# Four PSUM banks for the first y transposes, and one weight sum moved behind the scaling of chunk 12

## The chip, the core and the metric

The program runs on one core of a Trainium2 chip. The metric is the device time of one execution in microseconds (us); the median of the runs is what counts. The core has five engines that run their own instruction lists and meet at semaphores: TensorE (PE, matrix products and transposes into PSUM), VectorE (DVE), ScalarE (ACT), GpSimd (POOL) and SyncE (SP, which here only issues transfers).

## What is computed

One layer of a hybrid attention model on 256 tokens of width 2048, in float32. Cut to what the change touches:

```python
h = rmsnorm(x, g_norm)
proj = h @ w_in                      # q, k, v and gates of two attentions, and m_z, n_z
y_moba = rmsnorm(o_moba * silu(m_z), g_out_moba)   # 1024 columns, "half 0"
y_nsa  = rmsnorm(o_nsa  * silu(n_z), g_out_nsa)    # 1024 columns, "half 1"
y = concatenate([y_moba, y_nsa])
return rmsnorm(x + y @ w_out, g_final)
```

## The kernel before

**Products.** Each float32 product is made of three products of rounded operands: high by high, high by low, low by high (`three_products`, L647 to L649). So every block of weights is loaded by SP into one of three buffers of `w_raw`, rounded by ACT into `w_hi` (`hi`, L1022), and DVE then takes the rest into `w_lo` (`lo`, L1345). The weights are worked off in **units**: 512 rows of a chunk of 512 columns, for both halves of the tokens, 24 PE instructions of 512 columns. w_in has 15 chunks (0 to 14); w_out has 4, whose units start at number 56. A ring of three `w_hi`/`w_lo` buffers holds the rounded units, and ACT may round into one when PE has counted it as used.

**Slots.** PE, ACT and DVE each run through the same slots 0 to 75 in a loop; what an engine does in a slot, and in what order, stands in the loop's body. An engine runs ahead in its own list until a semaphore stops it. Chunks 11 to 14 (the z chunks) are worked in two pairs, (11, 12) from slot 44 on and (13, 14) from slot 52 on, with a scheme of seven block products in place of eight. Its operands are sums and differences of weight blocks, which DVE forms in `t1` to `t4`. `t4` of the second pair makes `blk_b11` from `blk_b21` (in the tile `wv`); ACT rounds it as block 6 (`block_hi`), DVE takes its rest (`block_lo`), and PE uses it in the last product of slot 53, P4.

**Around slots 51 to 53.** PE must not start the product P2 of chunk 14 into its banks before DVE has read chunk 12 out of the same banks. That is `scaled(12)`, two SCALAR_TENSOR_TENSOR instructions at L1561, after which `dve_read` lets `bank_free(14)` pass. In slot 51 DVE's order is: `t4`, `block_lo` 4, `block_lo` 5, `scaled(12)`. In slot 52 comes the `lo` of unit 51, and in slot 53 `block_lo` 6.

**The y rounds.** When a half of y has been scaled (`y_scale`, L1616), it is transposed in four rounds of four 128 by 128 transposes (`y_round_` on PE, L628, into one PSUM bank). DVE multiplies the bank by the gain into `pT` (`y_parts`, L1626, counts `yg_done`), ACT rounds it (`y_hi`, L1214), and DVE takes the rest (L1631, counts `ylo_done`). The rounds of half 0 are numbers 0 to 3; they stand in slots 55, 56, 57 and 58, and all four use the bank `b_t`, so that each waits until DVE has emptied it of the round before. Those of half 1 are numbers 4 to 7, in slots 62 and 63, in the banks `b_t`, `b_s`, `b_p`, `b_o`. Slot 58 has no unit on PE; slot 57 has unit 54, slot 59 unit 55, slot 60 unit 56. Unit 56 is the first of w_out and waits for all four rounds of half 0 (`ylo_done` 4).

The order on ACT and DVE in a slot is: round a unit of weights, then the slot's y rounds. The unit that is rounded in slots 55, 56, 57 and 58 is 54, 55, 56 and 57. DVE's `scaled(14)` and what follows from it (the sigmoid on ACT, a product of DVE, the product `xo` by z on POOL at L604, squares on ACT, `rstdy` on POOL, `y_scale(1)` on DVE) come in slots 59 to 61, and round 4 on PE in slot 62 waits for its end.

Of the kernel before, what the change touches and what calls it, by code (L numbers as in the profile page):

```python
# [20 lines left out]
S, D, P, HD = 256, 2048, 128, 128  # L21
MT = S // P
KT = D // P
NH = 8
HW = NH * HD
CW = 512
UK = 4
UPC = KT // UK
HPC = CW // HD
# [27 lines left out]
PAIRS = [(11, 12, 44), (13, 14, 52)]  # L57
# [124 lines left out]
ROUNDS = transpose_rounds()  # L182
# [20 lines left out]
JOBS = [(20 + 2 * h + i, "nsa", h, 1 - i) for h in range(8) for i in range(2)] + \  # L203
# [5 lines left out]
def score_reads(j):  # L209

    return 2 * (j + 1)
# [28 lines left out]
def heads_done(j):  # L240
# [10 lines left out]
CMP_SCORE_SLOT, CMP_TOKEN_SLOT, CMP_T_SLOT = [18, 26], [19, 27], [21, 31]  # L251
CMP_VALUES_AT = [0, 4]

Y_ROUNDS = {55: [(0, 0, 0)], 56: [(0, 0, 1)], 57: [(0, 1, 0)], 58: [(0, 1, 1)],
            62: [(1, 0, 0), (1, 0, 1)], 63: [(1, 1, 0), (1, 1, 1)]}
Y_NO = {r: n for n, r in enumerate(r for s in sorted(Y_ROUNDS) for r in Y_ROUNDS[s])}

# [8 lines left out]
def build_layer(nc, x, positions, inv_freq, w_in, g_norm, pe_ck, pe_cv, w_ck1, w_ck2, w_cv1, w_cv2,  # L266
# [4 lines left out]
    with ExitStack() as ctx:  # L271
# [7 lines left out]
        xo = sb("xo", [P, MT, D])  # L279
# [62 lines left out]
        b_s, b_o, b_t, b_p = bank("b_s"), bank("b_o"), bank("b_t"), bank("b_p")  # L342
# [29 lines left out]
        first_hi, quarters_ok, exp_done, pt_out, y_sq = sem("first_hi"), sem("quarters_ok"), sem("exp_done"), sem("pt_out"), sem("y_sq")  # L372
# [5 lines left out]
        s_read, negmax_ok, prob_ready, o_out = sem("s_read"), sem("negmax_ok"), sem("prob_ready"), sem("o_out")  # L378
        y_scaled, yg_done, ylo_done, ssf_ok, fin_dve = sem("y_scaled"), sem("yg_done"), sem("ylo_done"), sem("ssf_ok"), sem("fin_dve")
# [245 lines left out]
        def _(pe):  # L625
            def transpose4(bank_, srcs, done):
                for n, src in enumerate(srcs):
                    last = nc.tensor.transpose(bank_[:, n * P:(n + 1) * P], src, ident[:, :])  # L628
                last.then_inc(done, 1)
# [314 lines left out]
            def y_round_(r):  # L944
                half, hg, m = r
                n = Y_NO[r]
                if half == 0:
                    pe.wait_ge(y_scaled, m + 1)
                    if n == 0:
                        pe.wait_ge(t_out, len(ROUNDS))  # L950
                    bank_ = b_t
                    if n:
                        pe.wait_ge(yg_done, n)
                else:
                    pe.wait_ge(y_scaled, 2 + m + 1)
                    bank_ = (b_t, b_s, b_p, b_o)[n - 4]
                    if n == 4:
                        pe.wait_ge(yg_done, 4)
                transpose4(bank_, [xo[:, m, half * HW + (hg * HPC + h) * HD:half * HW + (hg * HPC + h + 1) * HD]
                                   for h in range(HPC)], y_round)  # L960

            def keep_busy(n):
# [370 lines left out]
        def _(dve):  # L1333
# [274 lines left out]
            def t4(p):  # L1608
                dve.wait_ge(blk_in[3], 16 * (p + 1))
                nc.vector.tensor_tensor(blk_b11, blk_b21, blk_b11, ALU.subtract).then_inc(blk_sum, 1)  # L1610
# [7 lines left out]
            def y_parts(r):  # L1618
                half, hg, m = r
                n = Y_NO[r]  # L1620
                bank_ = b_t if half == 0 else (b_t, b_s, b_p, b_o)[n - 4]
                dve.wait_ge(y_round, n + 1)
                dve.wait_ge(pt_out, len(JOBS))
                g0 = 16 + half * NH + hg * HPC
                yg = pT[:, n % 2, :].rearrange("p (h t) -> p h t", h=HPC)
                nc.vector.tensor_tensor(yg, bank_[:, :].rearrange("p (h t) -> p h t", h=HPC),  # L1626
                                        ccols[:, g0:g0 + HPC].unsqueeze(2).to_broadcast([P, HPC, P]), ALU.mult).then_inc(yg_done, 1)
                dve.wait_ge(yhi_done, n + 1)
                hi_, lo_ = ((ymT_hi, ymT_lo), (xT_hi, xT_lo))[half]
                sl = (slice(None), slice(hg * HPC, (hg + 1) * HPC), slice(m * P, (m + 1) * P))  # L1630
                nc.vector.tensor_tensor(lo_[sl], yg, hi_[sl].bitcast(F32), ALU.subtract).then_inc(ylo_done, 1)  # L1631
# [45 lines left out]
            for slot in range(NSLOT):  # L1677
                if slot == 0:
                    x_g(4)
                    x_g(5)  # L1680
                    first_lo_(1, [3])
                    first_lo_(2, [0])
                    x_lo(5)
                    first_lo_(2, [1, 2, 3])
                elif slot == 1:
                    x_g(6)
                    x_g(7)
                    lo(3)
                    x_lo(7)
                if slot == 38:  # L1690
                    x_sums()
                if slot == 40:
                    xs_residual()
                for p in range(len(PAIRS)):
                    s0 = PAIRS[p][2]
                    if slot == s0 - 4:
                        block_lo(p, 0)
                        t1(p)
                        block_lo(p, 1)
                    if slot == s0 - 2 and p:  # L1700
                        block_lo(p, 2)
                        block_lo(p, 3)
                        t3(p)
                    if slot == s0 + 1:
                        block_lo(p, 6)
                        if p:
                            z_times(PAIRS[p - 1][1])
                if slot > 1 and rounded_at(slot) is not None and rounded_at(slot) < NU:
                    lo(rounded_at(slot))
                if slot == PAIRS[0][2] - 2:  # L1710
                    block_lo(0, 2)
                    block_lo(0, 3)
                if slot == PAIRS[0][2] - 1:
                    t3(0)
                for p in range(len(PAIRS)):
                    if slot == PAIRS[p][2] - 1:
                        t4(p)
                for p in range(len(PAIRS)):
                    if slot == PAIRS[p][2] - 3:
                        t2(p)  # L1720
                if slot == 2:
                    dve.wait_ge(crows_T, 2)
                    nc.vector.tensor_copy(ccols[:, KT:], b_s[:, 0:80]).then_inc(cols_ok, 1)
                    dve.wait_ge(cols_ok, 2)
                    angles()
                if slot == 5:
                    tables()
                if slot in ROUNDS and ROUNDS[slot][0] == "kc":
                    kc_out(slot)
                if slot in ROUNDS and ROUNDS[slot][0] == "kv":  # L1730
                    k_residual(slot)
                if slot - 1 in ROUNDS and ROUNDS[slot - 1][0] == "raw":
                    nq_rope(slot - 1)
                if slot - 2 in ROUNDS and ROUNDS[slot - 2][0] == "raw":
                    q_residual(slot - 2)
                if slot - 1 in CMP_TOKEN_SLOT:
                    cmp_norm(CMP_TOKEN_SLOT.index(slot - 1))
                if slot - 1 in JOB_AT:
                    normalise(JOB_AT[slot - 1])
                if slot in EARLY_AT:  # L1740
                    early_lo(EARLY_AT.index(slot))
                if is_late(slot):
                    late_residual(slot)
                if slot % UPC == UPC - 1 and slot < NPROJ and KINDS[slot // UPC] in ROPED:
                    rope(slot // UPC)
                if slot - 3 in JOB_AT and ends_head(JOB_AT[slot - 3]):
                    o_evac(JOB_AT[slot - 3])
                if slot in JOB_AT:
                    row_max(JOB_AT[slot])
                for p in range(len(PAIRS)):  # L1750
                    if slot == PAIRS[p][2] - 1:
                        block_lo(p, 4)
                        block_lo(p, 5)
                if slot % UPC == UPC - 1 and slot < NPROJ and KINDS[slot // UPC] == "z":
                    scaled(slot // UPC)
                    if slot // UPC != PAIRS[0][1]:
                        z_times(slot // UPC)
                if slot in CK_SUM_SLOT:
                    hidden(CK_SUM_SLOT.index(slot))
                if slot == GATE_SLOT + 1:  # L1760
                    gates()
                if slot in CMP_TOKEN_SLOT:
                    cmp_shift(CMP_TOKEN_SLOT.index(slot))
                if slot in (54, 61):
                    y_scale((54, 61).index(slot))
                for r in Y_ROUNDS.get(slot, []):
                    y_parts(r)
                if slot in OUT_SLOT:
                    for m in range(MT):
                        residual(OUT_SLOT.index(slot), m)  # L1770
# [32 lines left out]
```

## Time and profile before

| | |
|---|---|
| Median of 3 runs | 502.27 us (502.1 to 502.31) |
| The profiled execution | 502.2 us |
| Its span, first to last instruction | 500.4 us |
| PE busy | 487.6 us, 97% of the span |
| PE loading weights | 404.8 us, 81% |
| DVE busy | 335.0 us, 67% |
| ACT busy | 250.5 us, 50% |
| POOL busy | 60.2 us, 12% |
| TensorE's granted clock, mean | 0.994 of full speed |

Times in the rows are microseconds from the span's start. A matmul's end is modelled, and neighbours overlap: an instruction of 512 columns is listed as 0.39 us long, while the next starts 0.23 us after it. So a gap is best read as the distance between two starts, less the usual distance. Idle time stands in square brackets with what ended it.

### The profile page before, as it was taken

How to read it: one execution, taken by the hardware profiler on the slowest of the kernel's cores; microseconds unless marked ns; L12 is line 12 of the kernel's file. 1: busy time of each engine (PE TensorE's matmuls, PEld its weight loads, DVE VectorE, ACT ScalarE, POOL GpSimd, SP SyncE). 2: the span in 40 equal slices, each digit the busy share in tenths (PEclk: the TensorE clock that was granted, in tenths of full speed). 3: DMA queues.
4: the chain of work that ended last, by engine and by line, in shares of the span. 5: the costliest groups of instructions: out<-in, count | busy, mean ns of one | idle time of the engine just before them, and what ended most of it. 6: DMA issues, size and time to landing. Idle time of an engine off the chain costs nothing.

```text
span 500.4 us, 6458 instructions
## 1 busy us (share of the span) xinstructions
PE 487.6 (97%) x2512; PEld 404.8 (81%) x2512; DVE 335.0 (67%) x535; ACT 250.5 (50%) x358; POOL 60.2 (12%) x66
## 2 busy tenths in 40 slices
PE   8999999999999999999999999999999899999993
PEld 7888778787788888888888888888878678888882
DVE  5886644345789949756688888577887656755442
ACT  5784335354556444564354384645864554445421
POOL 2340101001111202000020200002124040022020
PEclk9999999999999999999999999999999999999997
DMA  8979879685353442444344724274349565366222
GB/s 291 334 267 379 275 268 331 204 287 180 130 206 98 163 168 89 164 169 146 112 163 160 260 87 170 84 254 167 101 152 381 207 224 195 113 226 241 94 83 87
DMA packets 54544, 96.45 MB, mean 193 GB/s; under 512 B 4369, under 2 KB 13169, under 8 KB 54129
## 3 DMA queue, kind: packets, MB, share of 16 engines
q1 hardware_dynamic: 54480, 96.03, 55.2%
q8 instruction: 20, 0.33, 0.3%
q14 instruction: 12, 0.09, 0.1%
q10 hardware_dynamic: 32, 0.01, 0.0%
HBM read 93.93 MB, written 2.10 MB: 192 GB/s over the span
## 4 chain that ended last, share of the span: by engine, by line
PE 91%; issue 4%; ACT 2%; DVE 1%; DMA 1%; ACTq 0%; POOLq 0%; POOL 0%; DVEq 0%
PE proj L647 25%; PE proj L649 24%; PE proj L648 24%; PE b_o L941 4%; PE b_t L628 2%; PE b_p L910 2%; PE b_s L810 2%; PE proj L680 1%; PE proj L686 1%; PE proj L691 1%; ACT w_hi L1022 1%; DMA xo<-in_x_dram 1%; PE b_s L649 1%; PE b_s L647 1%; PE b_s L648 1%
## 5 line engine op out<-in xcount | busy, mean ns | idle before, releaser
L1345 DVE TENSOR_TENSOR w_lo<-w_raw,w_hi 128x2048 fp32r<-128x2048 f32 x68 | 156.9, 2310 | 90.7 <-ACT w_hi L1022 90.5
L647 PE MATMUL proj<-w_hi,xT_hi 128*128 128x512 f32 x484 | 191.0, 395 | 0.4 <-issue 0.4
L649 PE MATMUL proj<-w_hi,xT_lo 128*128 128x512 f32 x484 | 188.8, 390 | 0.0
L648 PE MATMUL proj<-w_lo,xT_hi 128*128 128x512 f32 x484 | 188.5, 390 | 0.0
L1022 ACT ACTIVATE w_hi<-w_raw 128x2048 fp32r<-128x2048 f32 x68 | 129.9, 1912 | 39.7 <-PE proj L649 28.3
L647 PEld LDWEIGHTS proj<-w_hi,xT_hi 128*128 128x128 f32 x484 | 90.9, 188 | 20.9 <-issue 2.4
L649 PEld LDWEIGHTS proj<-w_hi,xT_lo 128*128 128x128 f32 x484 | 90.9, 188 | 19.4
L648 PEld LDWEIGHTS proj<-w_lo,xT_hi 128*128 128x128 f32 x484 | 91.0, 188 | 17.8
L1159 ACT ACTIVATE pT<-b_p 128x512 f32<-128x512 f32 (+2 forms) x24 | 11.7, 489 | 53.9 <-PE b_p L910 53.9
L595 POOL TENSOR_TENSOR rope_a<-rope_a,rope_b 128x512 f32<-128x512 f32 (+1 forms) x12 | 13.1, 1111 | 160.0 <-DVE rope_b L1432 160.0
L647 PE MATMUL proj<-w_hi,ymT_hi 128*128 128x512 f32 x80 | 31.3, 392 | 0.6 <-DVE ymT_lo L1631 0.6
L649 PE MATMUL proj<-w_hi,ymT_lo 128*128 128x512 f32 x80 | 31.1, 389 | 0.0
L648 PE MATMUL proj<-w_lo,ymT_hi 128*128 128x512 f32 x80 | 31.1, 389 | 0.0
L1153 ACT ACTIVATE prob<-prob,nmx 128x256 f32<-128x256 f32 (+1 forms) x48 | 21.3, 448 | 7.7 <-DVE nmx L1528 7.7
L1524 DVE CUSTOM_DVE_ANT_0 prob<-b_s,mask 128x256 f32<-128x256 f32 (+1 forms) x48 | 15.2, 353 | 8.1 <-PE b_s L649 8.1
L647 PEld LDWEIGHTS proj<-w_hi,ymT_hi 128*128 128x128 f32 x80 | 15.0, 188 | 4.0 <-DVE ymT_lo L1631 1.0
L649 PEld LDWEIGHTS proj<-w_hi,ymT_lo 128*128 128x128 f32 x80 | 15.0, 188 | 3.2
L648 PEld LDWEIGHTS proj<-w_lo,ymT_hi 128*128 128x128 f32 x80 | 15.0, 188 | 3.0
L604 POOL TENSOR_TENSOR xo<-xo,rope_a 128x512 f32<-128x512 f32 x4 | 7.5, 1910 | 70.6 <-DVE xo L1548 64.0
L1135 ACT ACTIVATE Q<-b_t 128x512 f32<-128x512 f32 x9 | 5.4, 596 | 20.2 <-PE b_t L628 20.2
L617 POOL TENSOR_TENSOR Q<-Q,KV 128x512 f32<-128x512 f32 x6 | 7.6, 1294 | 61.0 <-ACT rope_c L1220 61.0
L582 POOL TENSOR_TENSOR rope_a<-rope_a,rope_b 128x512 f32<-128x512 f32 x4 | 6.2, 1548 | 67.4 <-DVE rope_b L1445 67.4
(249 smaller groups left out, 554.0 us busy)
## 6 DMA issues: line engine op xcount, KB each, us to landing
w_raw<-in_w_in_dram SPq DMA_DIRECT2D x53, 1024.0 KB, 4.9
w_raw<-in_w_out_dram SPq DMA_DIRECT2D x16, 1024.0 KB, 5.0
xo<-in_w_ck_dram SPq DMA_DIRECT2D x4, 1024.0 KB, 7.9
xo<-in_w_cv_dram SPq DMA_DIRECT2D x4, 1024.0 KB, 7.7
w_raw<-in_w_in_dram SPq DMA_DIRECT2D x12, 256.0 KB, 6.5
Q<-in_x_dram SPq DMA_DIRECT2D x1, 2048.0 KB, 9.9
out_dram<-Q SPq DMA_DIRECT2D x8, 256.0 KB, 2.9
xo<-in_x_dram SPq DMA_DIRECT2D x3, 512.0 KB, 7.6
```

Source lines behind the costliest of these rows:

```text
L595: nc.gpsimd.tensor_tensor(rope_a[:, m, 0:w], rope_a[:, m, 0:w], rope_b[:, m, 0:w], ALU.add).then_inc(rope_sum, 1)
L628: last = nc.tensor.transpose(bank_[:, n * P:(n + 1) * P], src, ident[:, :])
L647: nc.tensor.matmul(dst, a_hi, b_hi, start=first, stop=False, skip_group_check=goes_on)
L648: nc.tensor.matmul(dst, a_hi, b_lo, start=False, stop=False, skip_group_check=goes_on)
L649: return nc.tensor.matmul(dst, a_lo, b_hi, start=False, stop=last, skip_group_check=goes_on)
L810: last = nc.tensor.matmul(b_s[32 * j:32 * j + 32, kv * CH:(kv + 1) * CH], KV8[:, t0:t0 + CS * (TP - 1) + 1:CS], w[:, l8, :], start=l < 4, ...
L941: last = nc.tensor.matmul(b_o[:, m * P:(m + 1) * P], a, v, start=n == 0, stop=n == len(prods) - 1)
L1022: nc.scalar.activation(split_of(u)[0], w_raw[:, u % RAW], ACT.Copy).then_inc(hi_ready, 1)
L1153: last = nc.scalar.activation(prob[:, b, c0:c1], prob[:, b, c0:c1], ACT.Exp, bias=nmx[:, b, n:n + 1], scale=SCALE, accum_out=sums[:, b, n: ...
L1159: nc.scalar.activation(pT[:, j % 2, 0:width(j)], b_p[:, 0:width(j)], ACT.Copy).then_inc(pt_out, 1)
L1345: nc.vector.tensor_tensor(wl, w_raw[:, u % RAW], wh.bitcast(F32), ALU.subtract).then_inc(lo_ready, 1)
L1524: nc.vector.tensor_tensor_reduce(out=prob[:, j % 2, c0:c1], in0=b_s[:, c0:c1], in1=mask[:, slice(*mask_cols(j, n))], scale=1.0, scalar=NEG ...
```

## The change

Two places. The y rounds 1 and 2 both stand in slot 56, and round 3 in slot 57; all eight rounds take the banks `b_t`, `b_s`, `b_p`, `b_o` in turn, so that rounds 0 to 3 no longer wait for one another. Round 0 waits for the last readers of all four banks, and rounds 4 to 7 for the reader of the round four before. `t4(1)`, the sum of the second pair, moves on DVE from ahead of `block_lo` 4 to behind `scaled(12)`; `t4(0)` stays where it was.

```diff
-Y_ROUNDS = {55: [(0, 0, 0)], 56: [(0, 0, 1)], 57: [(0, 1, 0)], 58: [(0, 1, 1)],
+Y_ROUNDS = {55: [(0, 0, 0)], 56: [(0, 0, 1), (0, 1, 0)], 57: [(0, 1, 1)],
             62: [(1, 0, 0), (1, 0, 1)], 63: [(1, 1, 0), (1, 1, 1)]}
...
-                if half == 0:
-                    pe.wait_ge(y_scaled, m + 1)
-                    if n == 0:
-                        pe.wait_ge(t_out, len(ROUNDS))
-                    bank_ = b_t
-                    if n:
-                        pe.wait_ge(yg_done, n)
-                else:
-                    pe.wait_ge(y_scaled, 2 + m + 1)
-                    bank_ = (b_t, b_s, b_p, b_o)[n - 4]
-                    if n == 4:
-                        pe.wait_ge(yg_done, 4)
-                transpose4(bank_, [xo[:, m, half * HW + (hg * HPC + h) * HD:half * HW + (hg * HPC + h + 1) * HD]
+                pe.wait_ge(y_scaled, 2 * half + m + 1)
+                if n == 0:
+                    pe.wait_ge(t_out, len(ROUNDS))
+                    pe.wait_ge(s_read, score_reads(len(JOBS) - 1))
+                    pe.wait_ge(pt_out, len(JOBS))
+                    pe.wait_ge(o_out, 2 * NH)
+                if n >= 4:
+                    pe.wait_ge(yg_done, n - 3)
+                transpose4((b_t, b_s, b_p, b_o)[n % 4], [xo[:, m, half * HW + (hg * HPC + h) * HD:half * HW + (hg * HPC + h + 1) * HD]
...
-                for p in range(len(PAIRS)):
-                    if slot == PAIRS[p][2] - 1:
-                        t4(p)
+                    t4(0)
...
                     scaled(slot // UPC)
-                    if slot // UPC != PAIRS[0][1]:
+                    if slot // UPC == PAIRS[0][1]:
+                        t4(1)
+                    else:
                         z_times(slot // UPC)
```

On PE, before the change, at the end of slot 57 and in slot 58: the last products of unit 54, rounds 2 and 3, and the first product of unit 55 (x3 stands for the round's other three transposes).

```order
L649 MATMUL proj<-w_hi,xT_lo 128x512
L628 MATMUL b_t<-ident,xo 128x128 [waits yg_done,y_scaled]
L628 MATMUL b_t<-ident,xo 128x128 x3
L628 MATMUL b_t<-ident,xo 128x128 [waits yg_done,y_scaled]
L628 MATMUL b_t<-ident,xo 128x128 x3
L647 MATMUL proj<-w_hi,xT_hi 128x512 [waits lo_ready]
```

After the change, the pair of rounds that stands together is 1 and 2, a unit earlier, at the end of slot 56 (round 3 alone, in `b_o`, follows unit 54):

```order
L649 MATMUL proj<-w_hi,xT_lo 128x512
L628 MATMUL b_s<-ident,xo 128x128 [waits y_scaled]
L628 MATMUL b_s<-ident,xo 128x128 x3
L628 MATMUL b_p<-ident,xo 128x128 [waits y_scaled]
L628 MATMUL b_p<-ident,xo 128x128 x3
L647 MATMUL proj<-w_hi,xT_hi 128x512 [waits lo_ready]
```

The waits for `yg_done` are gone there, and the second of two neighbouring rounds writes another bank.

On DVE, before, from the rest of unit 55 (slot 56) to `scaled(14)` (slot 59): L1626 is a round's product with the gain, L1631 its rest, L1345 the rest of a weight unit.

```order
L1345 TENSOR_TENSOR w_lo<-w_raw,w_hi 128x2048
L1626 TENSOR_TENSOR pT<-b_t,ccols 128x512
L1631 TENSOR_TENSOR ymT_lo<-pT,ymT_hi 128x4x128
L1345 TENSOR_TENSOR w_lo<-w_raw,w_hi 128x2048
L1626 TENSOR_TENSOR pT<-b_t,ccols 128x512
L1631 TENSOR_TENSOR ymT_lo<-pT,ymT_hi 128x4x128
L1345 TENSOR_TENSOR w_lo<-w_raw,w_hi 128x2048
L1626 TENSOR_TENSOR pT<-b_t,ccols 128x512
L1631 TENSOR_TENSOR ymT_lo<-pT,ymT_hi 128x4x128
L1561 SCALAR_TENSOR_TENSOR rope_b<-proj,rstd,KV 128x512 x2
```

After (all lines of the file are four lower):

```order
L1341 TENSOR_TENSOR w_lo<-w_raw,w_hi 128x2048
L1622 TENSOR_TENSOR pT<-b_s,ccols 128x512
L1627 TENSOR_TENSOR ymT_lo<-pT,ymT_hi 128x4x128
L1622 TENSOR_TENSOR pT<-b_p,ccols 128x512
L1627 TENSOR_TENSOR ymT_lo<-pT,ymT_hi 128x4x128
L1341 TENSOR_TENSOR w_lo<-w_raw,w_hi 128x2048
L1622 TENSOR_TENSOR pT<-b_o,ccols 128x512
L1627 TENSOR_TENSOR ymT_lo<-pT,ymT_hi 128x4x128
L1341 TENSOR_TENSOR w_lo<-w_raw,w_hi 128x2048
L1557 SCALAR_TENSOR_TENSOR rope_b<-proj,rstd,KV 128x512 x2
```

Round 2 now stands ahead of the rest of unit 56, and round 3 ahead of the rest of unit 57, where before unit 56 stood ahead of round 2 and unit 57 ahead of round 3. ACT's list moves in the same way.

On DVE, slots 51 and 52, before:

```order
L1345 TENSOR_TENSOR w_lo<-w_raw,w_hi 128x2048 [waits hi_ready]
L1610 TENSOR_TENSOR blk_b<-wv,blk_b 128x1024 [waits blk_in3]
L1595 TENSOR_TENSOR w_lo<-raw_e,w_hi 128x1024 [waits blk_hi]
L1595 TENSOR_TENSOR w_lo<-wv,w_hi 128x1024 [waits blk_hi]
L1561 SCALAR_TENSOR_TENSOR rope_b<-proj,rstd,rope_b 128x512 [waits mid_out,unit_used]
L1561 SCALAR_TENSOR_TENSOR rope_b<-proj,rstd,rope_b 128x512
L1345 TENSOR_TENSOR w_lo<-w_raw,w_hi 128x2048 [waits hi_ready]
```

And after:

```order
L1341 TENSOR_TENSOR w_lo<-w_raw,w_hi 128x2048 [waits hi_ready]
L1591 TENSOR_TENSOR w_lo<-raw_e,w_hi 128x1024 [waits blk_hi]
L1591 TENSOR_TENSOR w_lo<-wv,w_hi 128x1024 [waits blk_hi]
L1557 SCALAR_TENSOR_TENSOR rope_b<-proj,rstd,rope_b 128x512 [waits mid_out,unit_used]
L1557 SCALAR_TENSOR_TENSOR rope_b<-proj,rstd,rope_b 128x512
L1606 TENSOR_TENSOR blk_b<-wv,blk_b 128x1024 [waits blk_in3]
L1341 TENSOR_TENSOR w_lo<-w_raw,w_hi 128x2048 [waits hi_ready]
```

The same six instructions stand between the same two neighbours; T4 (L1610, now L1606) has gone from first to last of them.

## Rows read from the trace of the kernel before

**Rows 1.** Waits of PE, 395 to 404 us: total, times, longest.

```profile
PE b_t L628 <- DVE pT L1626: 2.1, 1, 2.1
```

**Rows 2.** Timeline of PE, slots 57 to 60: start, length, what [idle before].

```profile
393.82 0.60 PE L628 MATMUL b_t<-ident,xo 128*128 128x128 f32 x4
396.55 0.63 PE L628 MATMUL b_t<-ident,xo 128*128 128x128 f32 x4 [2.12 <-DVE pT L1626]
396.93 0.48 PE L647 MATMUL proj<-w_hi,xT_hi 128*128 128x512 f32 x1
...
402.26 0.39 PE L649 MATMUL proj<-w_hi,xT_lo 128*128 128x512 f32 x1
403.24 0.50 PE L647 MATMUL proj<-w_hi,ymT_hi 128*128 128x512 f32 x1 [0.59 <-DVE ymT_lo L1631]
```

**Rows 3.** Timeline of PE, slot 53: products P7, P2 and P4.

```profile
364.55 0.39 PE L648 MATMUL proj<-w_lo,ymT_hi 128*128 128x512 f32 x1
364.77 0.39 PE L649 MATMUL proj<-w_hi,ymT_lo 128*128 128x512 f32 x1
365.54 0.47 PE L647 MATMUL proj<-w_hi,xT_hi 128*128 128x512 f32 x1 [0.38 <-issue]
...
369.73 0.39 PE L647 MATMUL proj<-w_hi,xT_hi 128*128 128x512 f32 x1
```

**Rows 4.** Timeline of DVE, slots 51 to 53.

```profile
360.63 1.22 DVE L1610 TENSOR_TENSOR blk_b<-wv,blk_b 128x1024 f32<-128x1024 f32 x1
...
362.90 1.22 DVE L1595 TENSOR_TENSOR w_lo<-wv,w_hi 128x1024 fp32r<-128x1024 f32 x1
364.04 1.40 DVE L1561 SCALAR_TENSOR_TENSOR rope_b<-proj,rstd,rope_b 128x512 f32<-128x512 f32 x2
365.36 2.28 DVE L1345 TENSOR_TENSOR w_lo<-w_raw,w_hi 128x2048 fp32r<-128x2048 f32 x1
367.56 1.22 DVE L1595 TENSOR_TENSOR w_lo<-blk_b,w_hi 128x1024 fp32r<-128x1024 f32 x1
```

**Rows 5.** Timeline of ACT: rounding of block 5 (slot 51) and block 6 (slot 53).

```profile
359.23 1.05 ACT L1084 ACTIVATE w_hi<-wv 128x1024 fp32r<-128x1024 f32 x1
...
365.79 1.05 ACT L1084 ACTIVATE w_hi<-blk_b 128x1024 fp32r<-128x1024 f32 x1
```

**Rows 6.** Timeline of PE, slot 62: rounds 4 and 5, in a row.

```profile
419.71 0.60 PE L628 MATMUL b_t<-ident,xo 128*128 128x128 f32 x4
420.15 0.60 PE L628 MATMUL b_s<-ident,xo 128*128 128x128 f32 x4
420.50 0.48 PE L647 MATMUL proj<-w_hi,ymT_hi 128*128 128x512 f32 x1
```

**Rows 7.** Timeline of DVE: rounds 1 and 3, then scaled(14).

```profile
390.32 0.68 DVE L1626 TENSOR_TENSOR pT<-b_t,ccols 128x512 f32<-128x512 f32 x1
...
401.12 0.68 DVE L1626 TENSOR_TENSOR pT<-b_t,ccols 128x512 f32<-128x512 f32 x1
402.50 0.69 DVE L1631 TENSOR_TENSOR ymT_lo<-pT,ymT_hi 128x512 fp32r<-128x512 f32 x1 [0.70 <-ACT ymT_hi L1214]
403.11 1.40 DVE L1561 SCALAR_TENSOR_TENSOR rope_b<-proj,rstd,KV 128x512 f32<-128x512 f32 x2
```

**Rows 8.** Timeline of DVE: y_scale(1), round 4, round 6.

```profile
415.26 1.41 DVE L1616 TENSOR_SCALAR xo<-xo,rstdy 128x1024 f32<-128x1024 f32 x2
...
420.35 0.69 DVE L1626 TENSOR_TENSOR pT<-b_t,ccols 128x512 f32<-128x512 f32 x1 [1.48 <-PE b_t L628]
...
427.75 0.69 DVE L1626 TENSOR_TENSOR pT<-b_p,ccols 128x512 f32<-128x512 f32 x1
```

**Rows 9.** Timeline of POOL: product with z of chunk 14.

```profile
405.40 5.06 POOL L604 TENSOR_TENSOR xo<-xo,rope_b 128x512 f32<-128x512 f32 x2 [17.97 <-DVE rope_b L1569]
```

**Rows 10.** Page, transfers: w_out's weight units, KB each, us to landing.

```profile
w_raw<-in_w_out_dram SPq DMA_DIRECT2D x16, 1024.0 KB, 5.0
```

**Rows 11.** Window: length, busy of PE, PEld, DVE, ACT, POOL; clock, DMA share, GB/s.

```profile
390.00:430.00 40.00, 37.28 (x176) 30.63 (x175) 26.03 (x26) 17.41 (x18) 6.13 (x5) 1.00 0.55 190
```

More of the change, by code:

```diff
@@ L1620, in y_parts @@
                 n = Y_NO[r]
-                bank_ = b_t if half == 0 else (b_t, b_s, b_p, b_o)[n - 4]
+                bank_ = (b_t, b_s, b_p, b_o)[n % 4]
                 dve.wait_ge(y_round, n + 1)
```

## The prediction

> **What bounds the kernel now.** I read the page first: PE is busy for 97% of the span, and the chain of work that ended last leads along PE nearly throughout. So the only time to be had is where PE stands still, and what DVE or ACT do elsewhere is free. The second view is the list of PE's waits. Beyond the start of the program it has three: one of 2.1 us for DVE in front of a y transpose [rows 1], one for `ylo_done` in front of the first unit of w_out, and one put down to nothing, as "issue". The third view is the timeline around them, for their true size. In [rows 2] round 2 starts at 393.82 and round 3 only at 396.55, since both use `b_t` and DVE empties it late; then unit 56 starts at 403.24, though the last product before it started at 402.26. In [rows 3] the gap before 365.54 is called issue, but the product there is P2, which needs `scaled(12)`. In [rows 4] that pair of instructions runs from 364.04 for 1.40, to 365.44, and P2 starts 0.10 later. It is a wait for DVE. The three waits are just where the change works.
>
> **The banks.** From round 2 to the first product of unit 55 PE needs 396.93 - 393.82 = 3.11 us [rows 2]. Two rounds in a row that don't wait for each other take 420.50 - 419.71 = 0.79 [rows 6], with the same transposes and two different banks. The number of rounds stays, so 3.11 - 0.79 = **2.32 us** go. The pair now stands after unit 53 and the single round after unit 54; that moves nothing on PE but their places. Round 0 gets three more semaphores to wait for, all long reached. The first product of unit 56 waits for four semaphores and starts at 403.24, 0.05 after `ymT_lo` ended (402.50 + 0.69) [rows 2, 7], so I take nothing for them, at most 0.05.
>
> **What is late next, at unit 56.** This unit wants `ylo_done` 4. Neighbouring products start 364.77 - 364.55 = 0.22 to 0.23 apart [rows 3], so it could have started at 402.26 + 0.23 = 402.49, and with the banks it could at 402.49 - 2.32 = 400.17. Is DVE through with round 3 by then? DVE and ACT do these steps in turn, and the new order (two rounds, a unit, a round) is the one that they already have in slots 62 and 63. There it takes from 420.35 to 427.75, 7.40 us, from the product with the gain of the pair's first round (4) to that of the round behind the unit (6) [rows 8]. Round 1's product starts at 390.32 [rows 7], and the banks change nothing in front of it. So round 3's starts at 390.32 + 7.40 = 397.72, its rest 402.50 - 401.12 = 1.38 later at 399.10, and PE may start 403.24 - 402.50 = 0.74 after that [rows 2, 7]: 399.84. That is 0.33 ahead of 400.17. So the wait goes too, and 403.24 - 402.49 = **0.75 us** with it.
>
> **T4.** It takes 364.04 - 362.90 = 1.14 us of DVE, as each of these block instructions does, from one start to the next [rows 4]. Behind `scaled(12)` it lets that pair start at 362.90 and end at 364.30. P2 could start at 364.77 + 0.23 = 365.00 [rows 3], so 365.54 - 365.00 = **0.54 us** go, with 0.70 to spare. Blocks 4 and 5 must be rounded 1.14 earlier for it: block 5's rounding on ACT ends at 359.23 + 1.05 = 360.28 [rows 5], before T4 even starts at 360.63. T4 itself would run from 365.36 - 1.14 = 364.22 to 365.44, and its reader on ACT, the rounding of block 6, starts at 365.79 [rows 5]. The rest of unit 51 starts at 365.36 as before. Last comes P4: it needs the rest of block 6, which ends at 367.56 + 1.22 = 368.78 [rows 4], and PE would ask at 369.73 - 0.54 = 369.19 [rows 3]: 0.41 to spare.
>
> **Nothing else takes it back.** The weights of unit 56 are done before round 3 on DVE (397.72), and wanted at 400.17. Unit 57's come behind round 3, and delay `scaled(14)`. A round costs DVE 403.11 - 401.12 = 1.99 [rows 7], so a unit and a round without it cost 7.40 - 1.99 = 5.41, and `scaled(14)` starts at 397.72 + 5.41 = 403.13, against 403.11 before. So the long way from there over POOL [rows 9] to `y_scale(1)` at 415.26 [rows 8] stays where it is, or comes 0.54 earlier if the whole stretch follows T4's gain, while PE arrives 3.61 earlier: at 416.10 for round 4 and at 420.15 - 3.61 = 416.54 for round 5 [rows 6]. The halves of y are ready at about 415.26 + 0.70 = 415.96 and 415.26 + 1.41 = 416.67 if nothing shifts. That would cost 0.13; with the shift it costs nothing. In the same way, if the chain of round 1 didn't follow T4's shift, unit 56 would lose 0.54 - 0.33 = 0.21. The load of unit 59 waits for the rest of unit 56, now done at 397.72; it lands in 5.0 us [rows 10], at 402.7, and its own rest is only taken ahead of 415.26 [rows 8].
>
> **The sum**: 2.32 + 0.75 + 0.54 = 3.61 us. The other end is the idle time in the brackets alone, 2.12 + 0.59 + 0.38 = 3.09 [rows 2, 3]; it leaves out the modelled ends of the products ahead, and distances between starts don't, so I take 3.61. The span goes from 500.4 to 496.8, the profiled execution from 502.2 to 498.6, and the median, 0.07 above that one, from 502.27 to 498.7.
>
> **Clock.** TensorE's granted clock is 1.00 through the stall and through rounds 4 to 7 in their four banks, the 2.4 GHz level in all of 390 to 430 [rows 11]. So the stalls cost no clock that could come back. The Trainium skill, "TensorE: Matmul & The Clock Gate", section "A second HAM failure mode: psum-queue depth-cycling", says that going round PSUM banks in turn can leave small idle pieces for which the clock swings between its levels. By that rule the change would be a loss; rounds 4 to 7 here, which already do it, don't show it.
>
> **The rivals.** (a) *A margin that isn't there.* At unit 56 it is 0.33, at P4 0.41, at round 5 at best 0.41. If one engine's step comes out longer by some tenths, or the issue gap isn't what I say and its 0.54 stays, the gain is 1.0 to 3.0 and the time 499.2 to 501.2, most likely near its lower end. For it speaks how thin the margins are, against it that the pattern of slots 62 and 63 is a measured one. (b) *The change does nothing*: DVE and ACT set the pace here, not the banks. They take 401.12 - 390.32 = 10.80 for two rounds further [rows 7], 5.40 a round, about a unit of PE. If round 3's rest came as late as before, PE would wait at unit 56 for what it no longer waits at round 3, and only 0.54 would be left: 501.7. Against it: taking round 2 ahead of unit 56's weights is what shortens this way by 401.12 - 397.72 = 3.40. (c) *Slower, over POOL*: PE's next point is round 5, which waits for the product with z on POOL, 5.06 us long [rows 9], and what follows. It decides from 0.41 us of delay on. If the new places of DVE's instructions made it wait and last twice as long, PE would lose 5.06 - 0.41 = 4.65, more than the 3.61: 503.3. Against it: DVE's order from `scaled(14)` on, and by the sum its time, stay. (d) *Slower, by the clock*: if the eight neighbouring transposes after unit 53 took it to 1.2 GHz for a unit, whose 24 products take 402.49 - 396.93 = 5.56 [rows 2], that unit would last up to 5.56 longer: 504.2. Against it [rows 11]. The rule named above is the one that would bring it.
>
> **Chances.** The forecast, 498.2 to 499.2: 0.81. (a): 0.12. (b) or another case within 0.2%: 0.03. (c) and (d): 0.02 each. A measurement of this kernel can tell about 0.2%, 1.0 us, from no change; so faster is 0.93, the same 0.03, slower 0.04. The range goes from 498.2, a little under the full sum, up to 500.2, which takes in 3.09 (499.2) and the better half of (a).
>
> **What the profile of the changed kernel would show.** PE's waits without the 2.1 and the 0.6 in front of the y rounds and unit 56, and no issue gap at P2. Rounds 1 and 2 together about 0.44 apart, in `b_s` and `b_p`. Round 3's product with the gain 7.4 us after round 1's. `scaled(14)` within half a microsecond of 403.1, and round 5 right behind round 4. The first product of unit 56 near 399.6. The forecast is wrong if PE waits anew at unit 56, P4, or rounds 4 and 5, and the size of that wait is what is missing.

## The result, and the profile after

The changed kernel takes 498.23 us in the median of 4 executions (498.18 to 498.54), the kernel before 502.29 in the same comparison: a ratio of 0.9918, with a 95% interval of 0.9901 to 0.9936. The forecast was 498.7 with 498.2 to 500.2. So it is faster, as predicted, by 4.1 us and not by 3.6; applied to the 502.27 from which the forecast started, the ratio gives 498.15, 0.05 below the lower end of the range. The interval of the ratio, 497.3 to 499.1 us, takes in the forecast of 498.7 and most of the range, so this comparison alone can't say that the sum was off; what it left out is read from the traces and from more executions below. The profiled execution took 498.54 (span 496.7), the slowest of the four; PE is now busy for 98% of the span.

The list of PE's waits (who waited for whom: total, times, longest) has one entry left, at the start of the program:

```profile
PE proj L961 <- POOL ident L551: 1.5, 1, 1.5
```

The timeline of PE, which answers to [rows 2] and [rows 3] (start, length, what, [idle before]):

```profile
365.00 0.39 PE L649 MATMUL proj<-w_hi,ymT_lo 128*128 128x512 f32 x1
365.22 0.39 PE L647 MATMUL proj<-w_hi,xT_hi 128*128 128x512 f32 x1
...
387.47 0.60 PE L628 MATMUL b_s<-ident,xo 128*128 128x128 f32 x4
387.90 0.60 PE L628 MATMUL b_p<-ident,xo 128*128 128x128 f32 x4
388.26 0.48 PE L647 MATMUL proj<-w_hi,xT_hi 128*128 128x512 f32 x1
...
393.81 0.60 PE L628 MATMUL b_o<-ident,xo 128*128 128x128 f32 x4
394.16 0.48 PE L647 MATMUL proj<-w_hi,xT_hi 128*128 128x512 f32 x1
...
399.51 0.39 PE L649 MATMUL proj<-w_hi,xT_lo 128*128 128x512 f32 x1
399.74 0.39 PE L647 MATMUL proj<-w_hi,ymT_hi 128*128 128x512 f32 x1
...
416.06 0.60 PE L628 MATMUL b_t<-ident,xo 128*128 128x128 f32 x4
416.50 0.60 PE L628 MATMUL b_s<-ident,xo 128*128 128x128 f32 x4
```

P2 follows P7 at 0.22, rounds 1 and 2 stand 0.43 apart, unit 55 starts behind round 3 without a stand, and unit 56 starts 0.23 after the last product of unit 55. Rounds 4 and 5 don't wait either. DVE's timeline, answering to [rows 4], [rows 7] and [rows 8]:

```profile
363.14 1.41 DVE L1557 SCALAR_TENSOR_TENSOR rope_b<-proj,rstd,rope_b 128x512 f32<-128x512 f32 x2
364.46 1.22 DVE L1606 TENSOR_TENSOR blk_b<-wv,blk_b 128x1024 f32<-128x1024 f32 x1
...
389.89 0.68 DVE L1622 TENSOR_TENSOR pT<-b_s,ccols 128x512 f32<-128x512 f32 x1
...
397.28 0.68 DVE L1622 TENSOR_TENSOR pT<-b_o,ccols 128x512 f32<-128x512 f32 x1
398.66 0.69 DVE L1627 TENSOR_TENSOR ymT_lo<-pT,ymT_hi 128x512 fp32r<-128x512 f32 x1 [0.70 <-ACT ymT_hi L1210]
...
402.68 1.40 DVE L1557 SCALAR_TENSOR_TENSOR rope_b<-proj,rstd,KV 128x512 f32<-128x512 f32 x2
...
414.84 1.41 DVE L1612 TENSOR_SCALAR xo<-xo,rstdy 128x1024 f32<-128x1024 f32 x2
```

The way from round 1 to round 3 takes 397.28 - 389.89 = 7.39 (predicted 7.40). With 0.74 from the start of its rest, PE could start unit 56 at 399.40, and comes at 399.74: a margin of 0.34 (predicted 0.33).

### The profile page after: what moved, and what is told of

The parts are those of the page before. It is cut to its first block, busy times and chain, and to the rows that moved or that the text cites. A ratio compares the mean times of both kernels' runs of the same rounds, so it can differ in the third digit from the quotient of the medians.

```text
span 496.7 us, 6459 instructions
## 1 busy us (share of the span) xinstructions
PE 487.2 (98%) x2512; PEld 405.4 (82%) x2512; DVE 335.6 (68%) x535; ACT 250.5 (50%) x358; POOL 60.9 (12%) x66
## 4 chain that ended last, share of the span: by engine, by line
PE 95%; issue 2%; DMA 1%; DVE 0%; ACT 0%; ACTq 0%; POOLq 0%; POOL 0%; DVEq 0%
PE proj L647 26%; PE proj L649 25%; PE proj L648 25%; PE b_o L941 4%; PE b_t L628 2%; PE b_p L910 2%; PE b_s L810 2%; PE proj L680 2%; PE proj L686 1%; PE proj L691 1%; DMA xo<-in_x_dram 1%; PE b_s L649 1%; PE b_s L647 1%; PE b_s L648 1%; PE b_p L628 0%
```

## Where the missing 0.4 us was

**Between the two profiles.** The start of the program differs by chance, so the two are compared from a common point. The pair of x rounds at 10.44 in the trace of before stands at 10.73 in that of after, 0.29 later; the first transfer of the output is issued at 484.29 before and at 480.66 after, 3.63 earlier. From the one point to the other, then, 3.92 us are won. Piece by piece (distances between starts): P7 to P2 0.77 - 0.22 = 0.55; round 0 to unit 55 14.95 - 12.61 = 2.34; unit 55 to unit 56 6.31 - 5.58 = 0.73. These are the three terms of the sum, 3.62 against 3.61. Two pieces that the sum took as unchanged are shorter as well: P2 to round 0 by 0.11 (16.44 to 16.33), unit 56 to round 4 by 0.15 (16.47 to 16.32). Their work is the same. They are the stretches behind a stand (a time in which PE has nothing that it may start). In the trace of before, the second products behind the stands that end at 365.54 [rows 3] and 403.24 [rows 2] are these, with the first transposes of round 0 and the first transfer of the output:

```profile
365.85 0.39 PE L648 MATMUL proj<-w_lo,xT_hi 128*128 128x512 f32 x1
...
381.98 0.60 PE L628 MATMUL b_t<-ident,xo 128*128 128x128 f32 x4
...
403.58 0.39 PE L648 MATMUL proj<-w_lo,ymT_hi 128*128 128x512 f32 x1
...
484.29 12.58 SPq L536 DMA_DIRECT2D out_dram<-Q  x8
```

And in the trace of after, round 0 and the first transfer:

```profile
381.55 0.60 PE L628 MATMUL b_t<-ident,xo 128*128 128x128 f32 x4
...
480.66 12.58 SPq L536 DMA_DIRECT2D out_dram<-Q  x8
```

The second products start 0.31 and 0.34 after the first, and not 0.23. That is 0.19 of the 0.26; the rest comes in the next few products, some of which start 0.24 apart. It isn't chance of these two traces. From P2 to round 0 it takes 16.42 to 16.46 in all six traces in which PE waits in front of P2, and 16.32 or 16.33 in all seven in which it doesn't. From unit 56 to round 4 it takes 16.46 or 16.47 in the three traces with a wait in front of unit 56 and the clock at its upper level, and 16.32 or 16.33 in the nine without a wait. Why the first products are slower stays open, and a stand isn't the only thing that brings it: behind rounds 1 and 2 in the trace of after, where PE never stood, the second product starts 0.31 after the first too (388.26 and 388.57).

That gives 3.88. The other 0.04 is chance: ahead of P7 the 0.29 shrinks to 0.23, and behind round 4 the way is 0.02 longer in the trace of after.

**In the start.** The profiled execution of after has its first products of real work 0.57 and 0.40 apart:

```profile
6.33 0.77 PE L680 MATMUL proj<-w_hi,xT_hi 128*128 128x512 f32 x1
6.90 0.57 PE L686 MATMUL proj<-w_hi,xT_lo 128*128 128x512 f32 x1
```

In the next profiled execution of the same kernel the first two are 0.31 apart, and its span is 0.2 us shorter:

```profile
6.19 0.47 PE L680 MATMUL proj<-w_hi,xT_hi 128*128 128x512 f32 x1
6.50 0.40 PE L686 MATMUL proj<-w_hi,xT_lo 128*128 128x512 f32 x1
```

The slower ones look like work at the lower level of the clock. But the window rows have a granted clock of 1.00 there in both executions, so this is argued from the distances and not shown.

**In the clock behind the stand.** This is the part that the prediction had excluded. Each execution comes with its mean granted clock. The kernel before was run 45 times beside the experiments. In 29 of them the mean is 0.994 or more, and their median is 502.21 us; in 16 it is 0.993 or less, and theirs is 502.81. Two more executions, profiled to see the difference, both had 0.992; they come last among the experiments. The mean is a rough sign, since it takes in the end of the program too: from 490 to 495 us, where PE has nothing left to do, the clock's row is 0.70 in the trace of after and 0.88 in the next one of the same kernel. So differences between 0.994 and 0.997 say nothing of the stands.

## The experiments

**The change again.** No edit.

> The changed kernel again, for the size of the gain. Theory A (the sum as predicted, 3.61 us, the rest is chance at the start of the program): the median is 3.6 us under that of the kernel before. Theory B (each stall also slows the first products behind it, some 0.1 us each, so the sum was 0.26 too small): 3.9 us or a little more under it; in the trace, from 10 us on, PE's last product has moved 3.9 us more than its products at 10 us have. No waits of PE from 350 us on, by both.

498.30 (498.09 to 498.85, 5 executions), ratio 0.9921 (0.9908 to 0.9933). With the four above, nine executions have a median of 498.27, and none has a mean clock under 0.994. Against the 502.21 of the kernel before at such a clock that is 3.94: theory B. Against its median over all 21 executions that stood beside the first four experiments, 502.38, it is 4.11. In the new trace the same two points are at 10.42 and 480.41, so 3.86 are won against the trace of before, by 0.25 more than theory A has and about what theory B has.

**Banks and slots, T4 where it was.** The lines on `t4` undone.

> Four banks and the new slots, with T4 where it was. Both theories: the waits in front of round 3 and of unit 56 are gone and the issue gap at P2 stays (0.38 idle, 0.54 by distance). Theory A: 3.07 us under the kernel before. Theory B: 3.2 to 3.3. Rival: if unit 56 waits anew because the margin there is only 0.3, under 3.0.

498.95 (498.85 to 499.12), 3.26 under 502.21: theory B again. PE's list shows the issue gap of 0.4 and nothing else from there on. So the two y terms are worth 3.26, T4 about 0.7.

**T4 alone.** The kernel before, with `t4(1)` behind `scaled(12)`.

> T4 behind scaled(12), with the y rounds as before. The issue gap at P2 goes and the waits in front of round 3 (2.1) and of unit 56 (0.6) stay, since the way of DVE and ACT behind scaled(13) follows PE. Theory A: 0.54 us under the kernel before. Theory B: 0.6 to 0.65. Rival: the way of DVE and ACT doesn't follow, the 0.54 comes back as a longer wait in front of round 3, and the time is that of the kernel before.

501.51 over 11 executions, ratio 0.9986 (0.9977 to 0.9995). They are of two kinds: eight with a clock of 0.994 or more, 501.33 to 501.72, so 0.7 under 502.21, and three with 0.991, 502.21 to 502.62, so 0.8 more in the median. The profile is of the second kind. PE behind its stand in front of round 3:

```profile
395.95 0.97 PE L628 MATMUL b_t<-ident,xo 128*128 128x128 f32 x4 [2.13 <-DVE pT L1626]
396.57 0.78 PE L647 MATMUL proj<-w_hi,xT_hi 128*128 128x512 f32 x1
397.14 0.63 PE L648 MATMUL proj<-w_lo,xT_hi 128*128 128x512 f32 x1
397.57 0.63 PE L649 MATMUL proj<-w_hi,xT_lo 128*128 128x512 f32 x1
```

The products start 0.43 apart and not 0.23, and the window rows have the clock at 0.50 from 397 to 399. T4's gain is kept (the rival, that it would come back as a longer wait, is out: the wait is 2.13 as before); what clouds it is the clock. The wait at unit 56, expected to stay, isn't in this trace either: the slower products have taken it in (unit 56 starts at 403.52, 0.23 behind the product ahead).

**Banks alone.** Four banks, T4 where it was, and

```diff
-Y_ROUNDS = {55: [(0, 0, 0)], 56: [(0, 0, 1), (0, 1, 0)], 57: [(0, 1, 1)],
+Y_ROUNDS = {55: [(0, 0, 0)], 56: [(0, 0, 1)], 57: [(0, 1, 0)], 58: [(0, 1, 1)],
```

> Four banks, but the rounds in their old slots 55 to 58, and T4 where it was. Theory 'order': the way of DVE and ACT (unit, round, unit, round) sets when round 3 is done, and the banks alone don't shorten it; the wait in front of round 3 goes, that in front of unit 56 grows from 0.6 to 2.9 idle (3.07 by distance), and the time is that of the kernel before, within 0.2 us. Theory 'banks': it was the one bank that held PE, and 2.3 us or more are won without the new slots.

502.36 over 11 executions, ratio 1.0009 (0.9998 to 1.002). The profile shows the wait moved whole:

```profile
394.30 0.60 PE L628 MATMUL b_o<-ident,xo 128*128 128x128 f32 x4
394.66 0.48 PE L647 MATMUL proj<-w_hi,xT_hi 128*128 128x512 f32 x1
...
403.28 0.50 PE L647 MATMUL proj<-w_hi,ymT_hi 128*128 128x512 f32 x1 [2.91 <-DVE ymT_lo L1627]
```

Round 3 no longer waits, unit 55 starts at 394.66, and unit 56 starts at 403.28, where it did before. The banks alone are worth nothing; theory "order" holds. Here too there are two kinds: six executions at 502.0 to 502.36 (clock 0.994 and more), five at 503.52 to 503.95 (0.991 to 0.993). Behind the longer stand the lower clock costs 1.6 in the median; no wait comes after it that would take it in.

**Slots alone.** The kernel before with the new `Y_ROUNDS`, all in `b_t`.

> The new slots (rounds 1 and 2 in slot 56, 3 in slot 57), but all in the one bank b_t with the waits as before, and T4 where it was. The way of DVE and ACT gets shorter by 3.4 us, and PE now stands 2.8 us in front of round 2, until DVE has emptied b_t of round 1; the wait at unit 56 falls from 0.75 to about 0.6 by distance. Theory 'order and banks together': 0.2 us under the kernel before, so 502.0 in executions in which the clock stays at its upper level. Theory 'clock': in several of the executions it falls behind that stand to the lower level, and these are 1 to 1.6 us slower, with a mean granted clock under 0.994. Rival 'order alone is enough': 2 us or more are won.

The stand is now in front of round 2:

```profile
388.24 0.60 PE L628 MATMUL b_t<-ident,xo 128*128 128x128 f32 x4
391.50 0.63 PE L628 MATMUL b_t<-ident,xo 128*128 128x128 f32 x4 [2.66 <-DVE pT L1626]
```

The median of the 11 executions is 503.09, ratio 1.0004 (0.9995 to 1.0013). Five take 501.88 to 502.29 (clock 0.995), six take 503.09 to 503.56 (0.992, 0.993). The wait at unit 56, expected at 0.6, is gone: the stand at round 2 is the only one of the y rounds. The trace is one of the five, and from round 1 (388.24) to the first transfer of the output (484.28) it has 96.04, against 96.40 from 387.89 to 484.29 before. So by the trace the slots alone save 0.36, which a later start of this execution hides; by the medians of the executions with the higher clock (502.15 and 502.11 against 502.21) either half of the change is worth 0.1 us or nothing, and both together 3.26. The lower clock costs 1.2 here; why less than with the banks alone no trace shows.

**The margin at unit 56, and a longer stand.** The changed kernel, with DVE's product of round 3 repeated:

```diff
+                for _ in range(3 if n == 3 else 0):
+                    link(nc.vector.tensor_tensor(yg, bank_[:, :].rearrange("p (h t) -> p h t", h=HPC),
+                                                 ccols[:, g0:g0 + HPC].unsqueeze(2).to_broadcast([P, HPC, P]), ALU.mult))
```

> The changed kernel, with DVE's product of round 3 made three times more (the same values each time), some 0.7 us each: it is 2.1 us late. If the margin at unit 56 is the 0.33 of the prediction, PE waits 1.8 us there by distance and everything behind moves by as much: 1.8 to 1.9 over the changed kernel, 500.1 to 500.2. If the margin were gone already, 2.1 or more. Theory 'clock': a stand of that length seldom lets the clock fall; where it does, another 1 us or more.

500.04 (499.70 to 500.18), 1.77 over 498.27. The three products put round 3's own off by 2.17 us (from 397.05 to 399.22), and PE waits

```profile
401.35 0.50 PE L647 MATMUL proj<-w_hi,ymT_hi 128*128 128x512 f32 x1 [1.69 <-DVE ymT_lo L1630]
```

1.69 idle, and 401.35 - 399.27 - 0.23 = 1.85 by distance from the product ahead. So the margin is 2.17 - 1.85 = 0.32, as predicted. The time can't measure it as well: the first transfer of the output is issued 2.07 later than in the second trace of the changed kernel (482.48 against 480.41), with 0.15 of it in the first products behind the stand, and from there to the end of the span it takes 15.62 in place of 16.09, for a reason that isn't known. None of the five executions has a clock under 0.995.

> As the one before, with eight more products in place of three: round 3 is 5.6 us late and PE stands 5.3 us at unit 56. Theory 'clock': behind a stand that long the clock is at its lower level in every execution, products start 0.43 us apart for some 3 us, and the time is 5.3 plus about 1.5, 505 or a little more; mean granted clock under 0.993 in all. Theory 'stalls cost no clock' (as predicted): 5.3 over the changed kernel, 503.6, and the clock row stays at 1.00.

505.28 (504.72 to 505.46), 7.0 over the changed kernel, of which the stand is 5.3. PE behind it, and the row of windows for the stretch after (length, busy of PE, PEld, DVE, ACT, POOL, then the granted clock):

```profile
404.91 0.80 PE L647 MATMUL proj<-w_hi,ymT_hi 128*128 128x512 f32 x1 [5.32 <-DVE ymT_lo L1630]
405.51 0.63 PE L648 MATMUL proj<-w_lo,ymT_hi 128*128 128x512 f32 x1
405.93 0.63 PE L649 MATMUL proj<-w_hi,ymT_lo 128*128 128x512 f32 x1
```

```profile
406.00:407.00 1.00, 1.00 (x4) 0.81 (x3) 1.00 (x1) 0.00 (x0) 0.00 (x0) 0.50 0.00 0
```

In the profiled execution the clock fell within the stand, with a row of 1.00 from 401 to 402 us and one of 0.50 from 403 to 404, and it is at its 1.2 GHz level when work comes back. From unit 56 to round 4 it takes 18.36 in place of 16.32, so 2.0 us are lost beside the stand of 5.47 by distance. The time shows 0.5 less than these two together, because the end of the span is shorter here as in the run before (15.63 from the first transfer on). Four of the five executions have a mean of 0.991 and one 0.994, where I had expected under 0.993 in all; that one is the fastest, at 504.72, and whether its clock fell is argued from its time alone.

**The start.** The changed kernel without `keep_busy(6)`.

> The changed kernel without the six products of the identity that PE makes from 1.5 us on, which nothing reads. For what the spread at the start of the program is: theory 'clock at the start': it comes up some 3 us later, the first products go at the lower level until about 9 or 10 us, and the time is 1 to 1.6 us over the changed kernel. Rival 'loads at the start': PE is held by its first loads and roundings anyway, and the time is that of the changed kernel within 0.3.

499.64 (499.39 to 500.14), 1.37 over the changed kernel. PE's first products:

```profile
6.34 0.77 PE L680 MATMUL proj<-w_hi,xT_hi 128*128 128x512 f32 x1
6.91 0.63 PE L686 MATMUL proj<-w_hi,xT_lo 128*128 128x512 f32 x1
7.34 0.63 PE L680 MATMUL proj<-w_hi,xT_hi 128*128 128x512 f32 x1
```

They start when they did, and the loads don't hide what they lose: the pair of x rounds comes at 11.55, and not at 10.73 or 10.42 as in the two traces of the changed kernel. The third product follows at 0.43, the distance that goes with a row of 0.50 behind the stands. The window rows have 1.00 here too, though, so that it is the clock is argued, and the price of 1.37 is what is shown.

**An earlier start of those products.** They work on 128 cleared columns of `rope_b`, from 0.97 us on, seven in place of six.

> The changed kernel, with PE's idle products at the start begun as soon as POOL has cleared 128 columns of rope_b (about 1.0 us instead of 1.5), seven of them in place of six. Theory 'clock at the start': the clock comes up half a microsecond earlier, before the first real products at 6.3 us, and the executions in which these go at the lower level are gone: all at 498.0 to 498.3, where the changed kernel had 498.09 to 498.85; median 0.1 to 0.2 under it. Rival: the start's spread comes from the loads, and the executions spread as before.

498.20 (498.14 to 498.40), ratio to the kernel before 0.9916 (0.9903 to 0.993). The spread is narrower than the 498.09 to 498.85 of the changed kernel, but the median differs by less than a measurement can tell, so whether it is a gain stays open.

**The kernel before, twice more.**

> The kernel before, for its trace alone. Theory 'clock': either the products behind the stand in front of round 3 start 0.23 us apart and the mean clock is 0.994 or more and the time about 502.2, or they start 0.43 apart for some 3 us, the mean clock is 0.992 or less and the time about 502.8. About one in three is of the second kind.

502.96, clock 0.992. This is the stand of [rows 2] again, in another execution:

```profile
396.67 0.63 PE L628 MATMUL b_t<-ident,xo 128*128 128x128 f32 x4 [2.12 <-DVE pT L1626]
397.05 0.48 PE L647 MATMUL proj<-w_hi,xT_hi 128*128 128x512 f32 x1
397.37 0.39 PE L648 MATMUL proj<-w_lo,xT_hi 128*128 128x512 f32 x1
...
397.83 0.59 PE L647 MATMUL proj<-w_hi,xT_hi 128*128 128x512 f32 x1
398.21 0.63 PE L648 MATMUL proj<-w_lo,xT_hi 128*128 128x512 f32 x1
398.64 0.63 PE L649 MATMUL proj<-w_hi,xT_lo 128*128 128x512 f32 x1
...
401.20 0.43 PE L649 MATMUL proj<-w_hi,xT_lo 128*128 128x512 f32 x1
...
404.20 0.39 PE L647 MATMUL proj<-w_hi,ymT_hi 128*128 128x512 f32 x1
```

The same wait to the hundredth, and a microsecond after its end the distance between products grows: 0.38, then seven of 0.42 or 0.43, then 0.28, which is 1.6 us more than at 0.23. Unit 56 no longer waits. The row of windows of this execution has the clock at 0.50 there, where [rows 11] had 1.00 throughout:

```profile
399.00:400.00 1.00, 1.00 (x4) 0.73 (x3) 0.98 (x1) 0.00 (x0) 0.00 (x0) 0.50 1.07 418
```

> The kernel before once more, for its trace alone; the same two kinds as in the run before this.

502.68, clock 0.992, and the same picture, with the slower products from 397.60 on and no wait at unit 56 (403.82).

## Why the prediction was right, and where it was not

**The three terms** were right: 2.32, 0.75 and 0.54 predicted, 2.34, 0.73 and 0.55 in the traces. Reading the issue gap of [rows 3] as a wait for `scaled(12)` was right, since moving T4 alone removes it.

**What is late next** was right: the way over slots 62 and 63 as the measure of the new order gave 7.40, and it is 7.39; the margin at unit 56 was 0.33, and is 0.34 in the trace and 0.32 by the slowed round. `scaled(14)`, `y_scale(1)` and rounds 4 and 5 came as worked out. Of the rivals, (a) fell with those margins. (b) fell for the change as a whole, and its reasoning was right for its halves: with the banks alone DVE and ACT set the pace, and the time stays.

**The failed step** is the sum of 3.61, which put two terms at nothing; the rest of it held.

The larger is the first products behind a stand. The sum took a gap as the distance to the first product's start, and the bracketed idle time as its other end; both leave out that the next product starts 0.31 or 0.34 later in place of 0.23. It measured 0.26 us, in two stretches of unchanged work.

The smaller is the clock, in the sentence "So the stalls cost no clock that could come back". It rested on [rows 11], one execution, and behind a stand of 2.12 us the clock falls in about one execution in three: 16 of 45 by their means, and both of the two profiled later. There it costs 0.60 in the median. In the trace, the slower products lose 1.6; the wait at unit 56, 0.75, takes in about half of that, and 0.15 more comes back because no stand is left there. That leaves 0.7: the way from the end of the stand to unit 56 is 7.53 (404.20 - 396.67) in place of 6.69 (403.24 - 396.55). The medians of the kernel before carry part of that, the changed kernel carries none. From 502.38, the median of the same 21 executions, to 502.21 is 0.17.

With both the sum is 3.61 + 0.26 + 0.17 = 4.04, and 4.06 lie between the two medians of the comparison. That they agree so well is in part luck: single executions of one kernel differ by 0.2 us and more at the start of the program alone, and in the four executions of the kernel before in that comparison the clock's share isn't known.

**The rival by the clock**, (d), had the sign the wrong way round: where the clock moves the time at all, the change wins by it. The Trainium skill, "TensorE: Matmul & The Clock Gate", section "A second HAM failure mode: psum-queue depth-cycling", speaks of banks in turn as a danger to the clock; here the rounds that go round four banks show no drop, in nine of nine executions by their means (0.994 and more), and in 15 of 15 of the three variants that keep these rounds and have no long stand at unit 56. Its section "HAM oscillation — how this bites in real kernels" speaks of waits that let the clock fall and of the time lost after them. With that these traces agree in kind: it was the wait for the one bank that put the clock at risk, and 2.12 us of it were enough in some executions and not in others. The lower end of the range, 498.2, lay 0.46 under the forecast's 498.66 and left just room for the 0.43 of both terms, but none for the spread.

## What to carry to other kernels

A wait in front of a shared buffer and the order of the work that empties it can each be worth nothing alone and three microseconds together: look at what is late next, and take a place in the same trace where the new order already runs as its measure. Price a stand of the tensor engine by more than its length: add the first products behind it, and ask over many executions, not one trace, whether the clock falls behind it. Here the mean granted clocks of the executions fell into two groups and their times with them (502.21 and 502.81), and without the stand the slower group was gone.

## What the runs showed of the hardware

How often the clock was lower behind a stand of PE, by the executions' mean clocks: none of 5 at 1.69 us idle, 16 of 45 at 2.12, 3 of 11 at 2.13, 6 of 11 at 2.66, 5 of 11 at 2.91, and 4 of 5 at 5.32, with the fifth by its time alone. Counts as small as these don't tell neighbours in this row from each other, so no limit can be drawn from them. These stands lie in the midst of work in which PE is otherwise never idle. The drop comes at different times: about a microsecond after work is taken up again in two executions (2.12 us), by the time it is taken up in another (2.13), and within the stand at 5.32. So a row of 1.00 in the stand itself says nothing. The whole loss was 0.6 to 0.8 us with a wait behind it to take part of it in, and 1.2 to 1.6 without one, in the medians. Apart from the clock, the stretch behind a stand took about 0.1 to 0.15 us longer than the same stretch without one, in every trace. At the start of the program, six products that nothing reads are worth 1.37 us.
